# State-space stage of a hybrid decoder step: swapped products replaced by VectorE operations across partition halves, Toeplitz matrices built by shifted copies

## The reference, cut to what matters

```python
bu_re = jnp.einsum('btgc,gpc->btgp', ug, bb_re)
bu_im = jnp.einsum('btgc,gpc->btgp', ug, bb_im)
...
def combine(e1, e2):        # over time
    a1r, a1i, b1r, b1i = e1
    a2r, a2i, b2r, b2i = e2
    return (a1r * a2r - a1i * a2i, a1r * a2i + a1i * a2r,
            a2r * b1r - a2i * b1i + b2r, a2r * b1i + a2i * b1r + b2i)
_, _, hr, hi = lax.associative_scan(combine, (a_re, a_im, bu_re, bu_im), axis=1)
y = (jnp.einsum('btgp,gcp->btgc', hr, c_re) - jnp.einsum('btgp,gcp->btgc', hi, c_im)
     + d.reshape(S5_GROUPS, S5_GROUP) * ug).reshape(B, T, S5_WIDTH)
```

## Time and profile before

| | us |
|---|---|
| median of 3 runs | 2369.13 |
| lowest, highest | 2362.12, 2372.32 |
| the profiled execution, its own time | 2369.92 |
| span of that execution in the profile | 2367.3 |
| TensorE busy | 2260.8 (95%) |
| VectorE busy | 1145.2 (48%) |
| ScalarE busy | 597.0 (25%) |
| GpSimd busy | 281.7 (12%) |

### The profile page before, as it was taken

The page is one execution under the profiler, slowest core; times in us unless marked ns, Lnnn a source line. Parts: engine busy times, 40 slices in busy tenths (PEclk is TensorE's granted clock), DMA queues, the critical chain, the costliest instruction groups (busy, mean ns, idle before and its releaser), DMA issues.

```text
span 2367.3 us, 34371 instructions
## 1 busy us (share of the span) xinstructions
PE 2260.8 (95%) x14712; PEld 2177.6 (92%) x14712; DVE 1145.2 (48%) x1264; ACT 597.0 (25%) x740; POOL 281.7 (12%) x436
## 2 busy tenths in 40 slices
PE   5799989999999999999999999999999999999995
PEld 5699978888989999999999998999999999999995
DVE  4716533334444344323654222437566655556665
ACT  4422233222322222233332124222111111111112
POOL 5989700000000000000000000000000000000000
PEclk9899999999989999999999999999999999999998
DMA  6311123121322222224322143111111111111111
GB/s 234 107 45 48 51 92 109 55 72 73 126 101 82 79 77 88 105 81 191 134 99 88 45 169 143 36 46 54 45 46 48 51 46 45 46 45 46 54 40 72
DMA packets 45221, 190.36 MB, mean 80 GB/s; under 512 B 5136, under 2 KB 5200, under 8 KB 41488
## 3 DMA queue, kind: packets, MB, share of 16 engines
q1 hardware_dynamic: 32112, 117.13, 14.4%
q0 software_dynamic: 11104, 54.41, 6.1%
q10 hardware_dynamic: 1872, 16.83, 1.8%
HBM read 152.59 MB, written 35.93 MB: 80 GB/s over the span
## 4 chain that ended last, share of the span: by engine, by line
PE 88%; issue 4%; DVE 3%; ACT 2%; POOL 1%; DMA 1%; DVEq 0%; ACTq 0%; POOLq 0%
PE ps L256 24%; PE ps L257 24%; PE ps L259 24%; PE ps L1715 1%; PE ps L1006 1%; PE ps L2043 1%; PE ps L2067 1%; DVE GT L399 1%; PE ps L371 1%; PE ps L372 1%; PE ps L374 1%; PE ps L2077 1%; POOL W L660 1%; PE ps L1691 0%; DVE WL L250 0%
## 5 line engine op out<-in xcount | busy, mean ns | idle before, releaser
L256 PE MATMUL ps<-XH,WH 128*128 128x344 f32 x1656 | 536.5, 327 | 8.5 <-DVE WL L250 6.0
L257 PE MATMUL ps<-XL,WH 128*128 128x344 f32 x1512 | 481.4, 322 | 0.0
L256 PE MATMUL ps<-XN,WH 128*128 128x344 f32 x1248 | 399.2, 322 | 4.3 <-issue 4.1
L257 PE MATMUL ps<-XN,WH 128*128 128x344 f32 x1248 | 397.2, 322 | 0.0
L250 DVE TENSOR_TENSOR WL<-WRAW,WH 128x1024 fp32r<-128x1024 f32 x175 | 220.3, 1260 | 309.3 <-ACT WH L245 308.2
L259 PE MATMUL ps<-XH,WL 128*128 128x344 f32 x1656 | 353.2, 322 | 0.0
L256 PEld LDWEIGHTS ps<-XH,WH 128*128 128x128 f32 x1656 | 314.8, 190 | 19.7 <-issue 14.4
L245 ACT ACTIVATE WH<-WRAW 128x1024 fp32r<-128x1024 f32 x175 | 184.3, 1054 | 534.6 <-PE ps L259 522.5
L257 PEld LDWEIGHTS ps<-XL,WH 128*128 128x128 f32 x1512 | 286.8, 190 | 0.2
L259 PEld LDWEIGHTS ps<-XH,WL 128*128 128x128 f32 x1656 | 279.4, 190 | 0.0
L259 PE MATMUL ps<-XN,WL 128*128 128x344 f32 x1248 | 264.3, 320 | 0.0
(11 more groups left out here) (512 smaller groups left out, 3165.9 us busy)
## 6 DMA issues: line engine op xcount, KB each, us to landing
WRAW<-in_wslabs SPq DMA_DIRECT2D x175, 512.0 KB, 3.5
scratch_spill<-STAGE SPq DMA_DIRECT2D x40, 516.0 KB, 2.6
ZS<-scratch_spill POOLq DMA_DIRECT2D x24, 516.0 KB, 5.5
XIN<-in_xT POOLq DMA_DIRECT2D x1, 4128.0 KB, 18.4
XR<-in_xT ACTq DMA_DIRECT2D x2, 2064.0 KB, 8.7
out_y<-XR SPq DMA_DIRECT2D x8, 516.0 KB, 3.0
CACHES<-in_ck ACTq DMA_DIRECT2D x4, 1024.0 KB, 14.2
CACHES<-in_cv ACTq DMA_DIRECT2D x4, 1024.0 KB, 15.6
```

The source lines that it names most:

```text
L256: pe.matmul(out[t], WH[:, slot, w, :], xh(k, t), start=(k == 0), stop=False)
L257: pe.matmul(out[t], WH[:, slot, w, :], xl(k, t), start=False, stop=False)
```

## The change

The second set of input products (`BT2`) and the permutation product (`PSW`) are gone. In their place DVE reads the operand from the one half of the partitions and writes it to the other: each product with `RS` becomes two instructions on 64 partitions, and the sign comes in by a `scalar_tensor_tensor` with a vector of +1 and -1 (`SGN`, `NSGN`). The shift products are gone too: SP copies `GK`, shifted, into eight slices of `TT`, which is set to zero once (its layout becomes `[t, g, c]`, so that a group's matrix is read in runs of 16). The fill steps are put elsewhere: a 1, b 2, c 5, d 4, f 2, g 2; point e is gone. In `dve_s5` the `WL` subtraction of fill c now stands ahead of `EP` times `RC`. The constants shrink by a fifth of `CF`.

```diff
 FILL = [(f"s{q}{p}", k) for q in range(4) for p, k in
-        (("a", 3), ("b", 2), ("c", 3), ("d", 2), ("e", 2), ("f", 2), ("g", 2))]
+        (("a", 1), ("b", 2), ("c", 5), ("d", 4), ("f", 2), ("g", 2))]
...
+            def toeplitz(q):
+
+                sp.wait_ge(s5_zero, 1)
+                sp.wait_ge(s5_act, s5_out("gk", q + 1))
+                for t in range(8):
+                    o_ = 16 * (7 - t)
+                    sp.dma_start(TT[0:128 - o_, t, :], GK[o_:128, :]).then_inc(tt_in, 16)
...
                 slab(j)
+                if j - 4 in FILL_SLAB:
+                    for q in range(4):
+                        if FILL_SLAB.index(j - 4) + 1 == filled(f"s{q}a") // KT:
+                            toeplitz(q)
+                elif j == FILL_SLAB[0] + 3:
+                    toeplitz(0)
...
-                nc.scalar.activation(BT2[:, :, 0:64], two(5)[:, :, 64:128], ACT.Copy, scale=-1.0).then_inc(s5_act, 1)
-                nc.scalar.activation(BT2[:, :, 64:128], two(5)[:, :, 0:64], ACT.Copy).then_inc(s5_act, 1)
...
-                act.wait_ge(s5_pe, s5_at("tt", q + 1))
-                nc.scalar.activation(TT[:, :, :].rearrange("p g (t c) -> p t g c", c=16),
-                                     two(3).rearrange("p t (g c) -> p t g c", c=16), ACT.Copy).then_inc(s5_act, 1)
...
+            nc.vector.memset(TT[:, :, :], 0.0).then_inc(s5_zero, 1)
...
-                tt(r4(T4[:, 0]), b2(3), r4(rc[:, :, :]), M)
-                tt(r4(T4[:, 1]), b2(5), r4(rs[:, :, :]), M)
-                tt(T4[:, 0], T4[:, 0], T4[:, 1], SU_)
+                part = lambda x, h: x[64 * h:64 * h + 64]
+                bu = ps[:, 3:5, :].rearrange("p a (g n) -> p a g n", n=128)
+                tt(r4(T4[:, 0]), bu, r4(rc[:, :, :]), M)
+                for h in range(2):
+                    tt(part(r4(T4[:, 1]), h), part(bu, 1 - h), part(r4(rs[:, :, :]), 1 - h), M)
+                L(nc.vector.scalar_tensor_tensor(out=T4[:, 0], in0=T4[:, 1], scalar=SGN, in1=T4[:, 0], op0=M, op1=AD))
...
                 dve.wait_ge(s5_scan, q + 1)
+                dve_fill(dve, f"s{q}c")
                 tt(T4[:, 0], EP[:, :, :], rc[:, :, :], M)
-                dve_fill(dve, f"s{q}c")
-                dve_fill(dve, f"s{q}d")
-                dve.wait_ge(s5_pe, s5_at("swap", q + 1))
-                tt(r4(T4[:, 1]), b2(5), r4(rs[:, :, :]), M)
+                for h in range(2):
+                    tt(part(T4[:, 1], h), part(EP[:, :, :], 1 - h), part(rs[:, :, :], 1 - h), M)
...
-                nc.vector.tensor_tensor(HST[:, :, 1:128], T4[:, 0, :, 0:127], T4[:, 1, :, 0:127], AD).then_inc(s5_h, 1)
+                nc.vector.scalar_tensor_tensor(out=HST[:, :, 1:128], in0=T4[:, 1, :, 0:127], scalar=NSGN,
+                                               in1=T4[:, 0, :, 0:127], op0=M, op1=AD).then_inc(s5_h, 1)
...
-                    pe.matmul(ps[:, 3 + g // 4, c], BT1[:, g, :], U[:, g, :], start=True, stop=True)
-                    last = pe.matmul(ps[:, 5 + g // 4, c], BT2[:, g, :], U[:, g, :], start=True, stop=True)
+                    last = pe.matmul(ps[:, 3 + g // 4, c], BT1[:, g, :], U[:, g, :], start=True, stop=True)
...
-                    last = pe.matmul(ps[:, 5 + k, :], PSW, EP[:, 4 * k:4 * k + 4, :].rearrange("p g n -> p (g n)"),
...
-                    last = pe.matmul(two(3)[:, t, :], SHIFT[:, 16 * (7 - t):16 * (7 - t) + 128], GK[:, :],
...
-                pe_fill(pe, f"s{q}e")
                 pe.wait_ge(s5_h, q + 1)
...
-                pe.wait_ge(s5_act, s5_out("tt", q + 1))
+                pe.wait_ge(tt_in, 128 * (q + 1))
...
-                    pe.matmul(ps[:, 3 + g // 4, c], U[:, g, :], TT[:, g, :], start=True, stop=False)
+                    pe.matmul(ps[:, 3 + g // 4, c], U[:, g, :], TT[:, :, 16 * g:16 * g + 16], start=True, stop=False)
```

More of the change, by code:

```diff
@@ L166, in cst @@
             return t
-        CF = cst("CF", [128, 5, 128])
-        IDENT, MASKNEG, ONES, PSW = (CF[:, k, :] for k in (0, 2, 3, 4))
-        SHIFT = CF[:, 0:2, :].rearrange("p a i -> p (a i)")
+        CF = cst("CF", [128, 4, 128])
+        IDENT, MASKNEG, ONES = (CF[:, k, :] for k in (0, 2, 3))
         LVL = cst("LVL", [128, LEVELS, 128], U8, 1)
@@ L537, in dve_mem @@
             dve_project(dve, SL_CK, 8)
-            dve.wait_ge(s5_den, 1)
+            dve.wait_ge(s5_red, 2)
             nc.vector.reciprocal(W(14), W(11)).then_inc(s5_rec, 1)
@@ L631, in program @@
         EP = USU
-        BT1, BT2 = nxt("BT1", [128, 8, 128]), nxt("BT2", [128, 8, 128])
+        BT1 = nxt("BT1", [128, 8, 128])
         TT, HST = nxt("TT", [128, 8, 128]), nxt("HST", [128, 8, 128])
@@ L652, in program @@
         s5_pe = sem("s5_pe")
-        s5_at = counts("tok", "bt", "gk", "u", "s", "st", "su", "swap", "tt", "ss", "y", "yt", "ys", "yst")
-        s5_stored = sem("s5_stored")
+        s5_at = counts("tok", "bt", "gk", "u", "s", "st", "su", "ss", "y", "yt", "ys", "yst")
+        s5_stored, tt_in = sem("s5_stored"), sem("tt_in")
         W = lambda k: W32[:, k, :] if k < 17 else WP[:, k - 17, :]
@@ L808, in act_s5 @@
                 else:
-                    act.wait_ge(s5_zero, 1)
+                    act.wait_ge(s5_zero, 2)
                     act.wait_ge(s5_tables, 1)
@@ L877, in dve_s5 @@
                 dve.wait_ge(s5_scan, q + 1)
+                dve_fill(dve, f"s{q}c")
                 tt(T4[:, 0], EP[:, :, :], rc[:, :, :], M)
-                dve_fill(dve, f"s{q}c")
-                dve_fill(dve, f"s{q}d")
-                dve.wait_ge(s5_pe, s5_at("swap", q + 1))
-                tt(r4(T4[:, 1]), b2(5), r4(rs[:, :, :]), M)
+                for h in range(2):
+                    tt(part(T4[:, 1], h), part(EP[:, :, :], 1 - h), part(rs[:, :, :], 1 - h), M)
                 if q:
                     dve.wait_ge(s5_pe, s5_at("y", q))
-                nc.vector.tensor_tensor(HST[:, :, 1:128], T4[:, 0, :, 0:127], T4[:, 1, :, 0:127], AD).then_inc(s5_h, 1)
+                nc.vector.scalar_tensor_tensor(out=HST[:, :, 1:128], in0=T4[:, 1, :, 0:127], scalar=NSGN,
+                                               in1=T4[:, 0, :, 0:127], op0=M, op1=AD).then_inc(s5_h, 1)
                 dve.wait_ge(s5_h, q + 1)
-                tt(SOUT[:, gs, 0], T4[:, 0, :, 127], T4[:, 1, :, 127], AD)
-                dve_fill(dve, f"s{q}e")
+                L(nc.vector.scalar_tensor_tensor(out=SOUT[:, gs, 0], in0=T4[:, 1, :, 127], scalar=NSGN,
+                                                 in1=T4[:, 0, :, 127], op0=M, op1=AD))
+                dve_fill(dve, f"s{q}d")
                 dve.wait_ge(s5_pe, s5_at("ss", q + 1))
@@ L955, in pe_s5 @@
                 pe_fill(pe, f"s{q}d")
-                pe.wait_ge(s5_scan, q + 1)
-                for k in range(2):
-                    last = pe.matmul(ps[:, 5 + k, :], PSW, EP[:, 4 * k:4 * k + 4, :].rearrange("p g n -> p (g n)"),
-                                     start=True, stop=True)
-                last.then_inc(s5_pe, 1)
-                pe.wait_ge(s5_act, s5_out("gk", q + 1))
-                for t in range(8):
-                    last = pe.matmul(two(3)[:, t, :], SHIFT[:, 16 * (7 - t):16 * (7 - t) + 128], GK[:, :],
-                                     start=True, stop=True)
-                last.then_inc(s5_pe, 1)
-                pe_fill(pe, f"s{q}e")
                 pe.wait_ge(s5_h, q + 1)
@@ L2569, in lay_out @@
     a["wplain"] = half(f["s5_w_glu"][0])
-    cf = z((128, 5, 128), np.float32)
+    cf = z((128, 4, 128), np.float32)
     r = np.arange(128)
```

12 lines of the change are left out of this document (4 added, 8 removed).

## The result

The changed kernel takes 2384.06 us (median of 7 runs, 2383.16 to 2387.02) where the kernel before takes 2372.32 (7 runs, 2362.12 to 2374.17). The ratio is 1.0062, with a 95% interval of 1.0049 to 1.0076: slower by 12 to 18 us, 11.7 between the two medians. I had forecast 2373.4 and no difference that can be measured; the time lies 0.06 us beyond the upper end of my range, 2384. The profiled execution took 2383.16 us, its span is 2381.3 us, 14.0 more than the 2367.3 of before.

A forecast was written before the change was run, and what follows sets the result against it. TensorE, busy 95% of the span, was taken to bound the kernel. 2369.9 - 8.3 (work gone) + 4.0 (later `HST`) + 7.8 (clock) = 2373.4 us, range 2361 to 2384 us.

The forecast's parts named there:

- Part 1: TensorE's input products halved and the wait for `BT2` gone: 2.07 us a batch, 8.3 us saved in four.
- Part 2: From fill c's end to L971, VectorE's chain to `HST` takes 12.5 us in three batches, 8.5 in the fourth: 4.0 lost.
- 5 x 2.05: Five VectorE operations in a row before L971, each 2.05 us beside GpSimd's work, in the first three batches.
- the dear crossing: Rival: each VectorE half product costs extra for crossing partitions; 2382.8 us at 0.6 us each; chance 0.12.
- the freedom from turns: Half products on 64 partitions exempt from turns with GpSimd: sum about 1.6 us a batch lower in three batches.
- Part 3: TensorE's clock falls behind the waits for `HST` in three batches: 7.8 us lost in all.
- 2.6 us each: Clock loss taken behind each of TensorE's three 5.5 us waits, from two waits elsewhere that lost 2.4 and 2.8.
- None for the 1.5 us one: No clock loss taken behind the fourth batch's 1.5 us wait of TensorE.
- Part 4: Hidden costs in the stage: `TT` transfers covered by over 18 us, zeroing and runs of 16: 0 us in the sum.
- clock stays up: Rival: TensorE's waits are there but cost only themselves; 2365.6 us; chance 0.14.
- No turns: Rival: GpSimd does not hold up the five VectorE operations, each batch like the fourth; 2353.6 us; chance 0.08.
- a tail: Tail of the main case: longer falls of the clock, 4 us each in four batches, slower by over 0.5%.

The follow-up runs named there:

- experiment 4: Changed kernel without GpSimd's table building for the second to fourth batch, all using the first batch's tables: 2362.20 us, ratio 0.997, stage 166.54 us.
- experiment 5: Changed kernel with the eight-column products put behind the output products instead of directly behind the wait for `HST`: 2381.73 us, ratio 1.0045, stage 184.68 us.
- experiment 1: Changed kernel with unneeded 128-column products on TensorE ahead of its wait for `HST`, to hold the clock: 2375.11 us, ratio 1.0033, stage 172.68 us.

## Why the prediction was right or wrong

**Part 1 (-8.3) was right.** The input products take 1.78 us (172.85 to 174.63, first batch), the wait for `BT2` is gone, and the balances that rest on 8.3 close within 0.6 us.

**Part 2 (+4.0) had the right mechanism and came out as +5.5.** The fourth batch was exact, 8.42 us against 8.5, with a wait of 1.24 against 1.5. The first was near, 13.03 against 12.5. The second was 15.20: the step that failed is "5 x 2.05", one length of a turn for all batches, taken from rows with GpSimd at 576 elements. The third was 10.94, shorter than I said, because the batch came later than I had assumed, and GpSimd finished in the middle of its chain (its last operation ends at 287.4, the chain at 293.5), so the last four operations had no turns. Nor is it ACT that starts the third chain, as I had taken it, but the scan, which ends 0.6 us after ACT's rounding. The longer turn was to be read from the trace of the kernel before, which has GpSimd operations of 1024 elements beside the second batch's chain (timeline):

```profile
236.05 2.82 POOL L741 TENSOR_TENSOR XP<-BB,PWD 128x1024 f32<-128x1024 f32 x1
```

The missing turns follow from my own longer batches, with the end of GpSimd's work at 287 us. That halves cost as much as wholes, that crossing is free and that they take turns like the rest was right; the dear crossing is ruled out by the 1.22 us above, the freedom from turns by the 1.84 us and by experiment 4. The Trainium skill, page "SBUF — State Buffer", section "Who interferes with whom", had said that two SBUF inputs are what makes the VectorE instruction contend; the trace agrees, 1836 ns with both in SBUF and 1222 ns with one in PSUM.

**Part 3 (+7.8) was mis-sized most: 13.8.** Two steps failed. "2.6 us each" came from waits with wide products behind them; here 8-column products follow and a fall costs 4.0, and with them moved away 2.2 on average (experiment 5), near my 2.6. That the narrow products make the difference is likely by that pattern and not shown. "None for the 1.5 us one" was wrong: 1.24 us took 1.7 us of clock, and in experiment 4 three of four such waits cost 1.7 to 3.4. The direction, that the clock falls behind these waits and that this is the price, stands (experiment 1).

**Part 4 had a hole: +3.4.** I wrote that moving two steps from a to c "costs nothing by itself". It took away the cover of `s5_done`, a wait that I did not look for because before it never showed: a fill of three steps hid it. Of the rest, the transfers, the stores behind them, the zeroing (0.9 us off the path) and the reads in runs of 16 cost nothing, as said.

Together: 1.5 + 6.0 + 3.4 = 10.9 us over the forecast; the stage grew by 13.8 where I had 3.5, 10.3 more, and the median lies 10.7 over. **The rivals:** "clock stays up" was made in experiment 1 and gave a stage of 172.7, where its sum of -4.3 asked for 170.0; the 2.7 between are the waits for `s5_done` and 0.3 of the chain. "No turns" was made in experiment 4, whose distances are the 8.4 us that it asked for, but it too forgot the clock. **The chances:** I gave slower by over 0.5% 0.16, too little, since most terms could grow more easily than shrink: a second kind of wait, a longer turn, a longer fall. These are not independent, as a longer wait comes with a longer fall. The fall of 4 us, which three batches had, stood in the forecast only as a tail.

## What to carry to other kernels

Before work is taken from an engine that sets the pace, list every wait that this work hides, those that never show in the profile too, and put the freed fill in front of the latest of them. Move an operation onto VectorE's critical path only with an operand in PSUM, or after looking at which GpSimd operations stand beside it and how long each is. Count a new wait of TensorE twice, once for itself and once for the clock, and try wide matmuls, not narrow ones, behind it.
